# A two-layer hybrid decoder trunk: opening, hooks and layer ends set beside main matmuls, recurrence and its gate computed features by tokens, rank weights' parts stationary together

## The reference

```
h    = rms_norm(x, norm_w)                      # 256 x 4096
proj = h @ w_in                                 # 4096 x (gla q,k,v | gla rank 16 | swa q,k,v | diff q,k,v | r_x | gate)
y    = concat(gla, swa, diff, lru) * silu(gate) # 4 x 1024 features
x    = x + y @ w_out
```

## Time and profile before

| | us |
|---|---|
| median of 3 runs (3003.4 to 3004.51) | 3003.53 |
| span of the profiled execution | 3002.7 |
| PE busy | 2944.2 (98%) |
| PEld busy | 2436.0 (81%) |
| DVE busy | 1606.2 (53%) |
| ACT busy | 1451.6 (48%) |
| POOL busy | 97.6 (3%) |

### The profile page before, as it was taken

One profiled execution on the slowest core, in us unless ns is written; L12 is line 12 of the kernel. 1 busy time (PEld: TensorE's weight loads), 2 busy tenths in 40 slices (PEclk: granted clock), 3 DMA queues, 4 the chain that ended last, 5 costly groups with the idle time before them and its releaser, 6 DMA issues.

```text
span 3002.7 us, 42098 instructions
## 1 busy us (share of the span) xinstructions
PE 2944.2 (98%) x13602; PEld 2436.0 (81%) x13602; DVE 1606.2 (53%) x2192; ACT 1451.6 (48%) x2125; POOL 97.6 (3%) x136
## 2 busy tenths in 40 slices
PE   6999999999999999999989999999999999999999
PEld 5888878888888887888878888788888888878887
DVE  6345555555666545444453454566656664454443
ACT  5334445455566545444453444455455665454443
POOL 1000000000000000000000000000000000000000
PEclk9999999999999999999999999999999999999999
DMA  7565555655555655666655555465655555666664
GB/s 247 166 192 169 160 158 182 184 174 180 178 164 164 184 186 175 217 219 201 212 176 166 188 164 167 149 191 176 186 178 175 161 168 176 194 191 202 216 218 161
DMA packets 283396, 549.23 MB, mean 183 GB/s; under 512 B 18776, under 2 KB 23072, under 8 KB 283328
## 3 DMA queue, kind: packets, MB, share of 16 engines
q1 hardware_dynamic: 270912, 524.35, 56.5%
q0 software_dynamic: 6048, 21.57, 2.1%
q10 hardware_dynamic: 6368, 2.48, 0.3%
HBM read 535.74 MB, written 12.58 MB: 183 GB/s over the span
## 4 chain that ended last, share of the span: by engine, by line
PE 97%; issue 1%; ACT 1%; ACTq 0%; DVE 0%; DMA 0%; DVEq 0%
PE main L1093 90%; PE mixer L1093 5%; PE mixer L1256 0%; PE mixer L1124 0%; DMA mix<-in_diff_lk 0%; ACTq L561 0%; ACT stage L402 0%; ACT w_hi L394 0%; PE mixer L1239 0%; PE mixer L1194 0%; PE mixer L1218 0%; PE mixer L1226 0%; PE mixer L1208 0%; PE mixer L1185 0%; PE mixer L1227 0%
## 5 line engine op out<-in xcount | busy, mean ns | idle before, releaser
L695 DVE TENSOR_TENSOR w_lo<-w_raw,w_hi 128x1024 fp32r<-128x1024 f32 x992 | 1193.2, 1228 | 1265.0 <-ACT w_hi L394 1264.1
L394 ACT ACTIVATE w_hi<-w_raw 128x1024 fp32r<-128x1024 f32 x992 | 1015.1, 1053 | 1313.1 <-PE main L1093 1308.4
L1093 PE MATMUL main<-w_hi,act_hi 128*128 128x512 f32 x3968 | 1580.2, 398 | 36.4 <-DVE act_lo L686 23.2
L1093 PE MATMUL main<-w_hi,act_lo 128*128 128x512 f32 x3968 | 1552.4, 391 | 0.0
L1093 PE MATMUL main<-w_lo,act_hi 128*128 128x512 f32 x3968 | 1549.8, 391 | 0.0
L1093 PEld LDWEIGHTS main<-w_hi,act_hi 128*128 128x128 f32 x3968 | 748.2, 189 | 192.3 <-issue 24.5
L1093 PEld LDWEIGHTS main<-w_hi,act_lo 128*128 128x128 f32 x3968 | 747.2, 188 | 159.4
L1093 PEld LDWEIGHTS main<-w_lo,act_hi 128*128 128x128 f32 x3968 | 748.6, 189 | 150.1
L686 DVE SCALAR_TENSOR_TENSOR act_lo<-act_T,par_now,act_hi 128x256 fp32r<-128x256 f32 x128 | 55.6, 479 | 11.2 <-ACT act_hi L383 11.0
L402 ACT ACTIVATE stage<-main,rstd 128x512 f32<-128x512 f32 x46 | 31.7, 688 | 57.4 <-PE main L1093 57.2
L383 ACT ACTIVATE act_hi<-act_T,par_now 128x256 fp32r<-128x256 f32 x128 | 56.8, 494 | 0.5 <-DVE par_now L1009 0.4
(11 more groups left out here) (229 smaller groups left out, 1218.8 us busy)
## 6 DMA issues: line engine op xcount, KB each, us to landing
w_raw<-in_w_in SPq DMA_DIRECT2D x736, 512.0 KB, 3.6
w_raw<-in_w_out SPq DMA_DIRECT2D x256, 512.0 KB, 4.0
mix<-out POOLq DMA_DIRECT2D x16, 512.0 KB, 6.2
out<-mix POOLq DMA_DIRECT2D x16, 512.0 KB, 3.6
mix_Y<-in_x SPq DMA_DIRECT2D x4, 1024.0 KB, 9.1
out<-mix_Y POOLq DMA_DIRECT2D x8, 512.0 KB, 8.1
act_T<-in_lru_w_r ACTq DMA_DIRECT2D x16, 64.0 KB, 2.1
act_T<-in_lru_w_i ACTq DMA_DIRECT2D x16, 64.0 KB, 2.3
```

Of the source, the lines that this page charges most:

```text
L394: act.activation(whi[:, g % RING, :, :], raw[:, g % RING, :, :], ACT.Copy).then_inc(w_hi, 1)
L695: dve.tensor_tensor(wlo[:, g % RING, :, :], raw[:, g % RING, :, :], whi[:, g % RING, :, :].bitcast(F32), ALU.subtract).then_inc(w_lo, 1)
L1093: return pe.matmul(out_, lhsT, rhs, start=start, stop=stop, skip_group_check=True)
```

## The change

- **Main loop.** All loops are written out (no hardware loops). `w_lo` has three buffers instead of four; ACT waits for each group by itself. At the end of each chunk PE waits for its own last matmul and then raises `main_ready`, which the evacuation of the second token half waits for.
- **Turned chunks.** The two r_x chunks and the last two gate chunks (7, 8, 21, 22) are computed features by tokens: 128x128 weight blocks are stationary, 256 tokens move (`turned_group`). DVE evacuates them, multiplied by a row of 1/rms (`take_turned`), which comes from one small matmul in chunk 1. The convolution and the scan work on that form directly, so LRU's four transposes per head and those of the last two gate chunks go.
- **Rank projection.** The hi and lo parts of the 16 rank weights stand side by side in a 128x32 stationary operand, act_hi and act_lo move as one operand of 512 columns; the sums are added later by DVE and by a doubled `gla_w_up`.
- **Opening.** Only `norm_w` and three groups' transposes come ahead of the first main matmul. The other 13 groups' transposes, splits and squares hang in hooks of chunk 0, and the parameters in chunk 1. x is not copied to the output buffer first.
- **Key norm, last gate, layer end.** The key norm and its transposes hang in chunk 7; the splits for w_out run during chunks 22 and 23; the splits for layer 1 during chunk 30 and chunk 0 of layer 1, in whose hooks 4 and 5 the last transposes of x stand. The last layer transposes and squares no new x.
- Evacuations go straight to their destination; POOL copies nothing.

```diff
-                for g in range(NG):
-                    pe.wait_ge(w_lo, n * NG + (g + 1 + RING))
-                    pe.wait_ge(a_lo, s * NG + (g + 2))
...
+            for layer in range(DEPTH):
+                for j in range(CHUNKS):
+                    for g in range(NG):
+                        n = group(layer, j, g)
+                        pe.wait_ge(w_lo_ready, n + 1)
+                        if j in (0, J_OUT):
+                            pe.wait_ge(a_lo, split_at(layer, j == J_OUT, g))
+                        ins = turned_group(layer, j, g) if j in TURNED else chunk_group(layer, j, g)
+                        ins.then_inc(w_used, 1)
+                        if g == NG - 1:
+                            pe.wait_ge(w_used, n + 1)
+                            pe.sem_inc(main_ready, 1)
+                        if j == 0 and layer == 0 and g + 3 < NG:
+                            turn_input(g + 3)
+                        if j == 0 and layer and g in (4, 5):
+                            turn_x(layer - 1, 7, g - 4)
+                        if j == 0 and g == NG - 1:
+                            rank(layer)
...
+            def turned_group(layer, j, g):
+                n = group(layer, j, g)
+                hi, lo = w_hi[:, n % HI, :, :], w_lo[:, n % LO, :, :]
+                for b in range(T):
+                    if g == 0:
+                        pe.wait_ge(main_free, n // NG * T - T + b + 1)
+                    for m in (2 * b, 2 * b + 1):
+                        o = main[b][:, (m % 2) * SEQ:(m % 2 + 1) * SEQ]
+                        cols = slice(m * P, (m + 1) * P)
+                        for k in range(KG):
+                            kt = KG * g + k
+                            mm(o, hi[:, k, cols], A[:, kt, 0, :], kt == 0 and m % 2 == 0, False)
+                            mm(o, lo[:, k, cols], A[:, kt, 0, :], False, False)
+                            ins = mm(o, hi[:, k, cols], A[:, kt, 1, :], False, kt == KT - 1)
...
-                for k in range(KT):
-                    o = M[1][0:RANK, 0:SEQ]
-                    mm(o, wa_hi[:, k, :], ahi[:, k, :], False, False)
-                    mm(o, wa_lo[:, k, :], ahi[:, k, :], False, False)
-                    ins = mm(o, wa_hi[:, k, :], alo[:, k, :], False, k == KT - 1)
+                        ins = mm(M[1][0:AR, :], wa[:, k, :], A[:, k, :, :].rearrange("p q n -> p (q n)"),
+                                 False, k == KT - 1)
...
+            def lo(layer, j, g):
+                n = group(layer, j, g)
+                dve.wait_ge(w_hi_ready, n + 1)
+                if n >= LO:
+                    dve.wait_ge(w_used, n - LO + 1)
...
+            def first_chunk(g):
+                if g < NG - 1:
+                    split_input_hi(g + 1)
```

More of the change, by code:

```diff
@@ L237, in from_in @@
[L237 to L244, removed]
-                             ).then_inc(x_in[i], 16)
[L246 to L252, removed]
-                    weight_chunk(n0 + i + O0, lambda g: w_out[
-                        layer, g * KG * P:(g + 1) * KG * P, ds(i * NC, NC)].rearrange(
-                            "(k p) n -> p k n", p=P))
@@ new lines, in _ @@
+            for layer in range(DEPTH):
+                for j in range(CHUNKS):
+                    for g in range(NG):
+                        if group(layer, j, g) >= RAW:
+                            weights(layer, j, g)
+            for t in range(T):
+                sp.wait_ge(x_added, DEPTH * 8 * T - T + t + 1)
+                sp.dma_start(out[0, t * P:(t + 1) * P, D - NC:D], x_new[:, t, :]).then_inc(end_stored, 16)
+            sp.wait_ge(end_stored, 16 * T)
+            sp.wait_ge(x_stored, 16 * (DEPTH * 8 - 1))
@@ L382, in a_split_hi @@
                 for k in range(KG * g, KG * g + KG):
[L383 to L384 removed]
+                    ins = act.activation(A[:, k, 0, :], F[:, k * SEQ:(k + 1) * SEQ], ACT.Copy,
+                                         scale=par[:, layer, base + k:base + k + 1])
                 ins.then_inc(a_hi, 1)
[L387 to L398 removed]
@@ L689, in a_split_lo @@
                 ins.then_inc(a_lo, 1)
-            def chunk(n, hooks=no_hooks, split=None):
-                for g in range(NG):
-                    dve.wait_ge(w_hi, n * NG + (g + 1))
-                    dve.tensor_tensor(wlo[:, g % RING, :, :], raw[:, g % RING, :, :],
-                                      whi[:, g % RING, :, :].bitcast(F32), ALU.subtract).then_inc(w_lo, 1)
-                    hooks(g)
-                    if split and g >= 1:
-                        for k in ((0, 1) if g == 1 else (g,)):
-                            split(k)
@@ L972, in _ @@
-            dve.wait_ge(par_act, 2)
-            chain = [20]
+                f = layer * 8 + i
+                n = layer * CHUNKS + i + J_OUT
+                dve.wait_ge(x_loaded, f * 16 + 16)
+                if f:
+                    dve.wait_ge(x_stored, f * 16)
+                if layer < LAST and i:
+                    dve.wait_ge(x_F, f * 2)
+                for t in range(T):
+                    dve.wait_ge(main_ready, n * T + t + 1)
+                    dve.tensor_tensor(x_new[:, t, :], x_old[:, t, :], main[t][:, :], ALU.add).then_inc(main_free, 1)
+                    dve.wait_ge(main_free, n * T + t + 1)
+                    dve.sem_inc(x_added, 1)
@@ L1090, in _ @@
+            add_x(LAST, 7)
         @block.tensor
```

1368 lines of the change are left out of this document (733 added, 635 removed).

## The result

The changed kernel takes 3026.58 us (median of four runs, 3025.8 to 3027.92), the kernel before 3004.02 beside it: ratio 1.0074, interval 1.0062 to 1.0086. The forecast was 2947.

The account below looks back on a forecast made before the run. The prediction took PE's matmuls, holding 97% of the chain of waits, as the bound; savings less losses made 56.2 us off 3002.7, so 2946.5, plus 0.8 for the median: 2947, range 2937 to 2957.

Parts of the forecast that it names:

- Smaller edits: Three w_lo buffers, moved hooks and written-out loops: cost nothing, or 0.5 us in each of 24 mixer chunks.
- The turned chunks: Eight chunks with 384 matmuls of 256 columns each, at 0.1135 us apiece, 43.6 us a chunk: nothing lost.
- Rival A: Weight loads cost a little: each turned matmul takes 0.120 us, 20 us more, 2967; chance 0.11.
- The opening: Start of the kernel: first main matmul near 9.5, chunk 1 at 69.8 instead of 94.27 us, 24.5 us saved.
- PE's own wait: At each chunk's end PE waits for its last matmul: 0.45 us at 50 ends, 22.5 us lost.
- rival D: At chunk ends PE's queue hides its own wait: 0.1 in place of 0.45 us, 17 less, 2930; chance 0.06.
- the tail: From the last matmul's end to the end of the span: 1.0 us saved, of 0 to 2.
- the stage ends: Stalls and cold clock go: 10.2 us at chunks 7 to 8, 12.8 at 22 to 23, 11.2 between layers.
- the hooks of the recurrence and gates: Transposes go from hooks: 7.2 us saved in the recurrence, 3.6 us in the last two gate chunks.
- Rival B: In turned chunks weight loads are not hidden: 235 us more at 0.19 us a matmul, 3182; chance 0.04.
- C: Support engines fall behind in the first chunk, opening and some mixer chunks: up to 15 us, 2960; chance 0.12.
- E: The opening doesn't shrink as written: all transfers of x must land first, 7 us more, 2954; chance 0.05.

Follow-up runs that it names:

- e1_align: The changed kernel with w_raw, w_hi and w_lo allocated ahead of mix_Y, nothing else changed: 2979.8 us, ratio to the kernel before 0.9922.
- b1_before_shift: The kernel before with par_now (640 bytes) allocated ahead of w_raw, which moves the weight buffers by 128 bytes: 3065.81 us, ratio 1.0201.
- c1_w64: e1_align with unused space added so that the weight buffers lie at a distance of 64 bytes from act: 2980.4 us.
- f1_half_load: e1_align with each turned stationary block cut to 64 of 128 columns, so half of the turned features are not computed: 2960.91 us.
- e4_open: The changed kernel with weights of groups 3 and 4 loaded ahead of x's fourth piece, groups 5 to 7 ahead of its fifth: 3019.29 us.
- e3_no_selfwait: The changed kernel without PE's wait for its own last matmul at chunk ends; readers of main1 wait for w_used instead: 3000.13 us.
- h1_lo_only: e1_align with 128 unused bytes between w_hi and w_lo, so that only w_lo is off: 3029.16 us.
- after: The changed kernel itself, against the kernel before: 3026.58 us, ratio 1.0074.

## Why the prediction was wrong

The direction was wrong, though nearly every removal came near what was worked out. The forecast of the span was 2946.5; it was 3024.1, 77.6 more, here in steps by way of e1_align:

- **Smaller edits, which were put at nothing: 47.7.** This is the step that failed. The prediction weighed the number of `w_lo` buffers and the length of the code, and took the pace of the main matmuls over from the earlier trace rows. It never asked where the buffers come to lie. The padding for the recurrence moved them by 128 bytes, and 226.7 became 232.4 to 233.3 ns (e1_align by spans: 3024.1 - 2976.4, of which some 0.6 us is its opening and not pace; b1_before_shift the other way round). The written-out code did cost nothing, as said.
- **The turned chunks: 20.** 0.1135 each was forecast; with the buffers back in place it was 0.1200, 3072 x 6.5 ns. Rival A had this number and its 20 us to the microsecond, and had a chance of 0.11. That was in part luck: its reason, loads that don't hide, can't stand alone, since full loads went by inside 113.3 in c1_w64; as far as f1_half_load shows, it was size and place together. The four transposes, float32 and with 128 moving columns, were a poor witness for these matmuls.
- **The opening: 6.** The first matmul came at 9.84 for 9.5. Then came a stall ahead of group 4 (6.0 and a cold stretch in the changed kernel, 3.3 in e1_align, where chunk 1 starts at 75.8 for 69.8), in the queue of SyncE, which the prediction counted only for the start. With e4_open chunk 1 starts at 70.6.
- **PE's own wait: 4.** 22.5 forecast, 26.5 measured with e3_no_selfwait: 0.53 in place of 0.45 per end: the first matmul is 0.46 late and the second 0.07 more. The mechanism was right, rival D wrong.

These are 77.7 of 77.6; what the small terms missed cancels (the tail gave 2.3 for 1.0). Right, therefore, were the stage ends (the rows at 425.53, 1157.62 and 1525.88 show only the 0.30 of the own wait), the hooks of the recurrence and gates, no clock fall after the opening, and the rank projection: 77.52 - 69.58 = 7.9 from its head to chunk 1, as forecast. Rival B had nothing to it, and of C only the late opening was there. E was right in part: the transfers of x did hold the opening up by about its 7 us, but ahead of group 4 and not ahead of the first matmul, and the stall there is the wait for `w_lo` inside a chunk that the prediction named as a sign against itself. None of the five had a pace slower in every plain chunk, and the range ended 59 us short.

The rule that a weight load overlaps only matmuls on other row groups (the Trainium skill, TensorE: Matmul & The Clock Gate, What overlaps and what doesn't) is not borne out by the runs: full loads of 128 columns went by inside 113.3 ns in c1_w64. The formula of the Trainium skill (TensorE: Matmul & The Clock Gate, Back-to-back issue gap) for an isolated matmul, N/2.4 + 2.5 ns, gives 216 and 109 ns; no mean pitch here went under 226.7 and 113.3, and the measurement decides.

## What to carry to other kernels

When a kernel is bound by TensorE's pace, the byte addresses of its operands are part of the design: list them before and after every edit that changes the size of any tensor allocated ahead of them, and keep the distance that the fast version had. Read the pitch from starts (or count matmuls in a fixed window), since the mean length barely moves. Price an edit "at nothing" only after asking what it moves in memory and in each queue.

## What the runs showed of the hardware

- The pace of fp32r matmuls hangs on the distance between the starts of the stationary and the moving buffers modulo 256 bytes, as far as tried: 226.7 ns per 512 columns at 0, 228.9 at 64, 232.4 to 233.4 at every other multiple of 32 tried; per 256 columns with the roles changed, 113.3 or 117.8 at 64 and 192, 120.0 at 0, 116.7 to 118.7 at the others. Other engines' work hardly bears on it: in plain chunks of the changed kernel the mean is 232.3 ns while DVE is busy throughout and 232.6 while it is idle.
- One buffer out of place slows the matmuls between its own as well (h1_lo_only), and a halved stationary block removes the loss of the turned ones at distance 0, 113.3 for 120.0 ns (f1_half_load). Why the distance counts stays open, and so does what picks between 113.3 and 117.8 after a hook or a chunk's start.
- TensorE that waits for its own last matmul loses 0.53 us each time: 26.5 us over some 50 chunk ends (after against e3_no_selfwait).
- A stall of 6.0 us in the opening left the granted clock at 0.50 for the seven matmuls after it (after, 26.54 to 33.36).
